# A hybrid GLA/Hyena layer with a mixture of experts: scale before shift, and the query between them

## The reference

```
mod = silu(cond) @ w_ada + b_ada            # w_ada: 2048 x 12288
sh1, sc1, gt1, sh2, sc2, gt2 = split(mod, 6)
h = rmsnorm(x, g_pre_mix) * (1 + sc1) + sh1
q, k, v, g, lr_f, lr_b, u_hy = split(h @ w_in)
la_f = log_sigmoid(lr_f @ w_dec_f + b) / 16      # likewise la_b
o = gla(q, k, v, la_f) + flip(gla(flip(...), la_b))   # chunks of 64, 4 heads
y_gla = rmsnorm(o) * silu(g);  y_hy = hyena(u_hy)     # long convolutions
x = x + gt1 * rmsnorm(concat(y_gla, y_hy) @ w_out, g_post_mix)
h = rmsnorm(x, g_pre_ffn) * (1 + sc2) + sh2
x = x + gt2 * rmsnorm(moe(h), g_post_ffn)        # 16 experts, top 2 of one group
```

## Time and profile before

| | |
|---|---|
| median of 3 runs | 1531.51 us (1527.08 to 1532.93) |
| profiled execution, its time | 1530.56 us |
| its span | 1528.7 us |
| PE busy | 1379.7 us (90%) |
| DVE busy | 748.8 us (49%) |
| ACT busy | 241.7 us (16%) |
| DMA traffic | 422.19 MB, mean 276 GB/s |
| mean granted PE clock | 0.965 |

### The profile page before, as it was taken

The page is one execution under the profiler, slowest core; times in us unless marked ns, Lnnn a source line. Parts: engine busy times, 40 slices in busy tenths (PEclk is TensorE's granted clock), DMA queues, the critical chain, the costliest instruction groups (busy, mean ns, idle before and its releaser), DMA issues.

```text
span 1528.7 us, 14045 instructions
## 1 busy us (share of the span) xinstructions
PE 1379.7 (90%) x5198; PEld 630.9 (41%) x5198; DVE 748.8 (49%) x1269; ACT 241.7 (16%) x401; POOL 75.1 (5%) x126
## 2 busy tenths in 40 slices
PE   2679999999999989999999999889989888798977
PEld 0135544444555545555544444543333333333322
DVE  0139889998677687978693752530000000000006
ACT  2110320100011111211121101521111101111104
POOL 3010000000001000000000001000000000000001
PEclk9689999999999999999999999989999999999999
DMA  9998458777549643322215844589999999999996
GB/s 345 424 359 254 170 173 276 249 259 254 165 144 339 222 146 109 117 69 90 83 55 213 289 157 170 235 351 427 427 426 394 430 427 428 426 386 427 427 424 279
DMA packets 134032, 422.19 MB, mean 276 GB/s; under 512 B 10253, under 2 KB 76024, under 8 KB 116852
## 3 DMA queue, kind: packets, MB, share of 16 engines
q1 hardware_dynamic: 120292, 375.79, 64.3%
q0 software_dynamic: 7584, 33.38, 6.0%
q10 hardware_dynamic: 6096, 12.20, 2.2%
HBM read 407.96 MB, written 22.58 MB: 282 GB/s over the span
## 4 chain that ended last, share of the span: by engine, by line
PE 74%; DMA 11%; DVE 8%; issue 3%; ACT 2%; ACTq 0%; POOL 0%; DVEq 0%; SPq 0%; POOLq 0%
PE ps L503 19%; PE ps L506 19%; PE ps L892 13%; PE ps L912 7%; DMA s_mem<-in_w_exp_gate 4%; PE ps L777 3%; DMA s_mem<-in_w_ada 3%; DMA s_mem<-in_w_exp_down 2%; DVE s_mem L1766 2%; PE ps L450 2%; PE ps L674 1%; DMA s_mem<-in_hy_freq 1%; PE ps L625 1%; PE ps L432 1%; DVE s_mem L1738 1%
## 5 line engine op out<-in xcount | busy, mean ns | idle before, releaser
L1592 DVE SCALAR_TENSOR_TENSOR s_mem<-s_mem,s_sT 128x512 f32<-128x512 f32 x480 | 339.4, 748 | 32.6 <-DMA s_mem<-in_w_ada 16.2
L503 PE MATMUL ps<-s_mem 128*128 128x384 f32 x1024 | 342.5, 492 | 1.1 <-DVE s_mem L1623 1.1
L506 PE MATMUL ps<-s_mem 128*128 128x512 f32 x672 | 292.8, 594 | 0.7 <-ACT s_mem L1366 0.7
L892 PE MATMUL ps<-s_mem 128*64 128x512 f32 x1152 | 256.4, 602 | 19.9 <-DMA s_mem<-in_w_exp_gate 18.7
L503 PEld LDWEIGHTS ps<-s_mem 128*128 128x128 f32 x1024 | 193.3, 191 | 142.5 <-issue 18.0
L506 PEld LDWEIGHTS ps<-s_mem 128*128 128x128 f32 x672 | 126.3, 190 | 158.5 <-issue 157.6
L892 PEld LDWEIGHTS ps<-s_mem 128*64 128x64 f32 x1152 | 87.4, 139 | 185.9 <-issue 185.9
L2059 DVE TENSOR_TENSOR s_mem<-s_mem,ps 64x512 f32<-64x512 f32 x18 | 12.2, 679 | 296.3 <-ACT s_mem L1461 296.3
L912 PE MATMUL ps<-s_mem 128*64 128x512 f32 x576 | 144.2, 659 | 9.3 <-DVE s_mem L2061 9.3
L1262 ACT ACTIVATE s_mem<-ps 128x512 f32<-128x512 f32 (+1 forms) x61 | 34.4, 581 | 316.3 <-PE ps L506 154.0
L912 PEld LDWEIGHTS ps<-s_mem 128*64 128x64 f32 x576 | 43.7, 150 | 96.4 <-issue 84.6
(11 more groups left out here) (287 smaller groups left out, 1025.0 us busy)
## 6 DMA issues: line engine op xcount, KB each, us to landing
s_mem<-in_w_ada SPq DMA_DIRECT2D x256, 256.0 KB, 3.2
s_mem<-in_w_exp_gate SPq DMA_DIRECT2D x32, 2048.0 KB, 21.1
s_mem<-in_w_exp_up SPq DMA_DIRECT2D x32, 2048.0 KB, 25.4
s_mem<-in_w_exp_down SPq DMA_DIRECT2D x32, 2048.0 KB, 24.4
s_mem<-in_w_in SPq DMA_DIRECT2D x24, 2048.0 KB, 8.8
s_mem<-in_w_ada SPq DMA_DIRECT2D x16, 2048.0 KB, 12.5
s_mem<-in_w_out SPq DMA_DIRECT2D x8, 2048.0 KB, 8.2
y_slots<-s_mem ACTq DMA_DIRECT2D x34, 256.0 KB, 11.1
```

The source lines that it names most:

```text
L503: m = mm(ps[:, banks[m_], 0:TOK], v[:, k, m_ * P:(m_ + 1) * P], hT[:, kk, :], start=(kk == 0), stop=(kk == KT - 1))
L506: m = mm(ps[:, banks[m_], :], hT[:, kk, m_ * P:(m_ + 1) * P], v[:, k, :], start=(kk == 0), stop=(kk == KT - 1))
L892: m = mm(ps[half, 0, :], hgT[:, kh * 8 + k, :], weights(e, 2 * kh + which)[:, k, :], start=(kh + k == 0), stop=(kh * 8 + k == KT - 1), ski ...
L1592: v.op(ve.scalar_tensor_tensor(out=o, in0=w, scalar=scale, in1=o, op0=ALU.mult, op1=ALU.add), S("piece_used") if last else None)
```

## The change

Scale and shift are separated. The scale comes first, in two halves of 1024 columns (four slots each, 4 k tiles by 1024 columns); then the shift in eight slots of 2 k tiles by 2048 columns. The query's two weight halves go to places of their own (`wq`) and no longer through the ring. PE multiplies the query weights with tokens that are scaled but not shifted, between the steps of the scale's second half and of the shift; the part of the query that comes from the shift is a separate product of the shift's columns with the query weights (`qshift`), turned to columns (`colQ`) and added by ACT as a bias when it copies the query out. The first half of the key now stands ahead of `lr`, and the decay products lie inside its second half. DVE scales tokens in two parts and adds the shift in a second pass. `run(26)` is gone; the pieces start after ring load 16 (the key's first half), and 13 more pieces stand among the loads of the output projection. The token loads come first on ACT's queue.

PE, new and changed:

```diff
-            pe.wait_ge(S("sT_ready"), 2)
-            for k in range(KT):
-                ada_step()
...
+            def scale_step(h, r):
+                cols = SCALE * D + 2 * h * NCOL
+                w = next_slot(pe, w_ada[4 * r * P:4 * (r + 1) * P, cols:cols + 2 * NCOL].rearrange("(k p) n -> p k n", p=P))
...
+            def shift_step(a):
+                w = next_slot(pe, w_ada[2 * a * P:2 * (a + 1) * P, SHIFT * D:(SHIFT + 1) * D].rearrange("(k p) n -> p k n", p=P))
...
+            def q_products(m_, kts):
+                for kt in kts:
+                    if m_ == 0:
+                        pe.wait_ge(S("h_scaled"), kt + 1)
+                    m = mm(ps[:, m_, 0:TOK], wq[kt // 8][:, kt % 8, m_ * P:(m_ + 1) * P], hT[:, kt, :],
+                           start=(kt == 0), stop=(kt == KT - 1))
+                return m
+
+            pe.wait_ge(S("sT_ready"), 2)
+            scale_step(0, 0)
+            scale_step(0, 1)
+            pe.wait_ge(S("x_scaled"), NT)
+            for kt in range(KT):
+                x_turn(kt)
+                if kt in (4, 9):
+                    scale_step(0, 2 + kt // 9)
+            scale_columns(0)
...
+            pe.wait_ge(S("in_q0"), 16)
+            for m_ in range(4):
+                take(pe, m_, f"q_{m_}", ("act",))
+                m = q_products(m_, range(8))
+                scale_step(1, m_)
+            m.then_inc(S("q_read"), 1)
+            shift_step(0)
+            scale_columns(1)
+            shift_step(1)
...
+            pe.wait_ge(S("in_q1"), 16)
+            for m_ in range(4):
+                m = q_products(m_, range(8, 12))
+                if m_ % 2 == 1:
+                    shift_step(2 + m_ // 2)
+            m.then_inc(S("q_read"), 1)
+            for m_ in range(2):
+                q_products(m_, range(12, KT)).then_inc(filled(f"q_{m_}"), 1)
+                shift_step(4 + m_)
+            shift_step(6)
+            shift_step(7)
+            q_products(2, range(12, KT)).then_inc(filled("q_2"), 1)
+            wait_read(pe, "dve", "shift")
+            mod_columns(SHIFT, 5)
+            q_products(3, range(12, KT)).then_inc(filled("q_3"), 1)
...
-            project("q", "fm", w_in, COL_Q)
-
+            where_k = ("k", "fm", w_in, COL_K)
+            project_half(*where_k, 0, between=q_shift_columns, banks=(4, 5, 7, 0))
+
+            pe.wait_ge(S("h_shifted"), KT)
             pe.wait_ge(S("in_lr"), 16)
-            take(pe, 4, "lr", ("act",))
+            take(pe, 3, "lr", ("act",))
...
+            def decay_products():
+                wait_read(pe, "act", "lr")
...
+                        if h % 2 == 1:
+                            yield
+
+            project_half(*where_k, 1, banks=(4, 5, 7, 0), turn=decay_products())
```

Where the sums stand, and SP:

```diff
-        ADA_SUMS = {("q", 1): 0, ("k", 1): 1, ("v0", 1): 2, ("v1", 0): 3, ("v1", 1): 4, ("g0", 0): 5, ("g0", 1): 6,
-                    ("g1", 0): 7, ("g1", 1): 8, ("hy00", 1): 9, ("hy01", 1): 10, ("hy10", 0): 12,
-                    ("wo1", 0): 13, ("wo2", 0): 14, ("wo2", 1): 15}
-        PIECES_AFTER = {1: 8, 2: 8, 3: 3, 4: 6, 5: 4, 6: 7, 7: 7, 8: 8, 9: 9, 10: 7, 11: 5, 12: 4, 13: 6, 14: 4,
-                        15: 6, 16: 4, 17: 8, 18: 2, 20: 2, 22: 2, 24: 2, 25: 4, 27: 4, 28: 6, 29: 2}
+        ADA_SUMS = {("v0", 0): 0, ("v0", 1): 1, ("v1", 0): 2, ("v1", 1): 3, ("g0", 0): 4, ("g0", 1): 5, ("g1", 1): 6,
+                    ("hy00", 1): 7, ("hy01", 1): 8, ("hy11", 0): 10, ("wo1", 0): 11, ("wo1", 1): 12, ("wo2", 0): 13,
+                    ("wo2", 1): 14}
+        PIECES_AFTER = {16: 4, 17: 1, 18: 3, 19: 5, 20: 7, 21: 8, 22: 9, 23: 9, 24: 8, 25: 5, 26: 4, 27: 6, 28: 4,
+                        29: 6, 30: 4, 31: 8, 32: 2, 34: 2, 36: 2, 38: 2, 39: 6, 40: 4, 41: 6, 42: 5, 43: 5, 44: 3}
...
+            def load_q(kh):
+
+                if kh == 1:
+                    sp.wait_ge(S("x_scaled"), NT)
+                sp.dma_start(wq[kh], w_block(w_in, kh * 8 * P, COL_Q)).then_inc(S(f"in_q{kh}"), 16)
...
-                if i == 0:
-                    small_loads()
-                for _ in range(PIECES_AFTER.get(i - KT, 0)):
+                if i in Q_LOAD_AFTER:
+                    load_q(Q_LOAD_AFTER[i])
+                for _ in range(PIECES_AFTER.get(i, 0)):
                     load_piece()
```

In the old table the keys count from the query's first half, in the new one from the list's start: new key n stands where old key n - 14 stood. `Q_LOAD_AFTER` is `{3: 0, 7: 1}`, and `small_loads` now comes before the list. DVE:

```diff
-            run(26)
...
-            mod_chunk(0)
             run(14)
...
-            mod_chunk(1)
             run(20)
+            mod_chunk(0)
+            mod_chunk(1)
+            run(16)
             mod_chunk(2)
             run(16)
             mod_chunk(3)
             mod_row(2)
+            run(20)
+            mod_chunk(4)
             run(16)
-            mod_chunk(4)
-            run(20)
             mod_chunk(5)
-            run(16)
-            mod_chunk(6)
             run(4)
...
-            mod_chunk(13)
+            run(10)
+            mod_chunk(11)
             mod_columns(3, 0)
...
                 if nb == 1:
-                    for _ in ada:
-                        pass
+                    run(16)
+                    mod_chunk(12)
+                if nb == 2:
+                    mod_chunk(13)
+                    run(6)
...
+                    if nb == 2 and t < 2:
+                        run(5)
```

More of the change, by code:

```diff
@@ L77, in shape_constants @@
     lower = (np.arange(P) >= BLK)[:, None]
-    base = np.concatenate([ident, tri, sel.reshape(P, 2 * P), total, np.tile(rows, (P, 1)), tokens, lower], 1).astype(np.float32)
+    shifts = np.zeros((P, 32), np.float32)
+    for j in range(4):
+        for c in range(2):
+            shifts[32 * j + 2 + c, c] = 1
+    base = np.concatenate([ident, tri, sel.reshape(P, 2 * P), total, np.tile(rows, (P, 1)), tokens, lower, shifts], 1).astype(np.float32)
     masks = np.zeros((P, 2, P), np.int32)
@@ new lines, in _ @@
+            for kt in range(KT):
[3 more added lines that the diff above has]
+            scale_columns(0)
+            pe.wait_ge(S("in_rowsB"), 32)
+            take(pe, 4, "colB")
+            tr(ps[:, 4, 0:96], rowsB, ident[0:96, 0:96]).then_inc(filled("colB"), 1)
+            pe.wait_ge(S("in_mlp"), 16 * 9)
+            take(pe, 3, "hid1")
+            mm(ps[0:HID, 3, 0:TOK], w1s, pe_sb, start=True, stop=True).then_inc(filled("hid1"), 1)
@@ new lines, in _ @@
+            wait_read(pe, "dve", "shift")
+            mod_columns(SHIFT, 5)
+            q_products(3, range(12, KT)).then_inc(filled("q_3"), 1)
+            wait_read(pe, "dve", "modT0")
+            take(pe, 6, "qshift", ("act",))
+            for k in range(KT):
+                j = k % 4
+                m = mm(ps[32 * j:32 * j + 32, 6, :], sT[:, k, :], wq[k // 8][:, k % 8, :], start=(k < 4),
+                       stop=(k >= KT - 4), skip_group_check=True)
+            m.then_inc(filled("qshift"), 1)
@@ L495, in project_half @@
                         take(pe, banks[m_], bk, readers)
-                    if m_ == 2 and between:
+                    if m_ == (1 if key == "k" else 2) and between:
                         between()
@@ L693, in _ @@
                 if ho == 0:
-                    project_half(*where, 0, both, turn=hy_turn(0, 1, (7, 7, 7), 11))
+                    project_half(*where, 0, both, turn=hy_turn(0, 1, (7, 7, 7), 9))
                 else:
@@ L785, in _ @@
             out_last(0, 1)
+            ada_sum(15)
             out_last(1, 0)
@@ L1212, in load @@
                 act.dma_start(dst, src).then_inc(S(sem), 16)
+            for t in range(NT):
+                load(x_sb[:, t, :], x_rows[t], f"in_x{t}")
             load(rowsB[0:72, :], T["hy_conv_w"][0].rearrange("j (m p) -> (j m) p", p=P), "in_rowsB")
@@ L1222, in _ @@
                 load(dst, src, "in_mlp")
-            for t in range(NT):
-                load(x_sb[:, t, :], x_rows[t], "in_x")
             wait_read(act, "dve", "colA")
@@ new lines, in _ @@
+            inverse_roots(0, NT)
+            for t in range(NT):
+                v.op(ve.tensor_scalar(h_tm[:, t, :], x_sb[:, t, :], stat[:, t:t + 1], None, ALU.mult), S("x_scaled"))
+            dve.wait_ge(S("in_rows"), 16 * 10)
+            scale_tokens(0)
+            b = read(dve, "colB")
+            v.op(ve.tensor_copy(colB[:, :], ps[:, b, 0:96]), freed("dve", "colB"))
+            dve.wait_ge(S("in_mlp"), 16 * 9)
+            sine_argument("hid1", 0, HID)
+            scale_tokens(1)
@@ L1628, in _ @@
+                for c, toks in both:
+                    v.op(ve.tensor_scalar(hT[:, kt, toks], hT[:, kt, toks], sT[:, kt, 2 + c:3 + c], None, ALU.add),
+                         S("h_shifted") if c == 1 else None)
             for d in range(2):
@@ L1839, in _ @@
             gla_head(2)
-            mod_chunk(9)
+            mod_chunk(7)
             gla_head(3)
```

215 lines of the change are left out of this document (116 added, 99 removed).

## The result

The changed kernel takes 1561.2 us (median of 4 runs, 1558.9 to 1563.0); the kernel before took 1529.95 beside it. The ratio is 1.0203, 95% interval 1.0186 to 1.0221: 31 us slower, where 1530 and a range of 1516 to 1543 had been predicted. The direction and the range were both wrong.

The account below looks back on a forecast made before the run. Transfers were taken to bound the prologue, then DVE's chain from the last decay product to the first head. Terms: -0.1 us at the head, -1.2 in the output projection, -1.3 in all; forecast 1530 us, range 1516 to 1543.

Parts of the forecast that it names:

- E: Moment when the last decay product ends on PE; predicted at 164.8 us, against 161.9 in the kernel before.
- the head: Start of `g1`'s second half, beside which the first linear-attention head runs; predicted at 359.8 us, against 359.9 before.
- The 35 us of my last section: Expected trace sign: PE idle at L432, released by L1592, some 35 us between E and the head.
- The 4.9 us wait: DVE's one long idle, for an exponential queued behind the last key copy; predicted to go.
- the slower rival: In the prologue, PE waits for scaled tokens and the query starts at 54.5; 1539 to 1540 us, chance 0.22.
- an ada step is 1.92 us at the higher clock, 3.6 at the lower: Price per ada step on PE in the prologue, set by PE's clock.
- the prologue is a transfer: Claim that loads of 33.5 MB bound the prologue; last shift load taken at 107.3 us.
- the tail to the key: PE's work from the last shift load to the key's start; predicted 9.7 us, key at 117.
- PE waits at `ada_sum`, blocked until its chunk is ready: Between E and the head, PE's own work is 157 us and it waits for DVE's chunks.
- DVE is idle during the key instead, some 40 us: DVE idles some 40 us beside the key, since pieces begin only after the last decay product.
- The first rival: DVE's chain does not set the head, PE does: head at 334.8, 25 us earlier, 1504 us; chance 0.10.
- my own last paragraph: Expected trace signs, among them the key's first matmul at 117 us (109 to 126).

Follow-up runs that it names:

- e4_low_rank_in_key: Changed kernel with the low-rank product after the key's first block and decay products after its next blocks; 1546.8 us.
- e1_four_groups: Changed kernel with the scale step alternating over all four 32-column groups, DVE adding the second partial sum; 1551.4 us.
- e2_bank_freed_early: Changed kernel with `mod_chunk(0)`, which frees the PSUM bank, ahead of `run(20)` instead of behind it; 1555.7 us.
- e5: As e3, with the first value third `v0` accumulating in banks 3, 1 and 2 instead of 0, 1 and 2; 1515.4 us.
- e7_queries_ahead_of_last_loads: As e5 plus the four-group scale step of e1_four_groups, and the last two query pieces ahead of the last two shift steps; 1503.1 us.
- e3: Changed kernel with 26 `w_ada` steps and their loads moved ahead of and between the decay additions, and `mod_chunk(0)` early; 1528.9 us.

## Why the prediction was wrong, step by step

**Right.** DVE's chain from E sets the head in the main (e4_low_rank_in_key moved E by 14.9 and the head by 15.6). DVE idles beside the key: it waited 45.2 us at L1742, 29.6 of them at once. PE waits at the ada sums in its place: 24.8 us in three waits before the head. (The 35 us of my last section don't fit my own sum: 195.0 less PE's own 157 leaves 38, of which 13 were the `v0` load's.) The `v0` load comes at E + 14.8 (13 predicted). Chunk 0 is complete at E + 39.9 (39.6 predicted). The 4.9 us wait ahead of the key preparation is gone. The tokens did not gate the query, so the slower rival named the wrong mechanism: all tokens were scaled at 24.8 us (23 to 25 predicted). The query began at 47.0, the edge of what I had allowed, because PE was busy with slow steps until then. The output projection hid its 26 additional steps; this is DVE ahead of its last block, where 10 us of slack had been predicted:

```profile
973.17 0.69 DVE L2001 TENSOR_TENSOR s_mem<-s_mem,ps 128x512 f32<-128x512 f32 x1 [9.95 <-PE ps L852]
```

**The failed step: "an ada step is 1.92 us at the higher clock, 3.6 at the lower".** I read the 3.59 us of the earlier trace rows as the clock's (granted 0.52 in 98.9 to 102.4 us, 1.00 in 62.7 to 64.6) and gave the scale's new step 1.92, without looking on which partitions it writes. Both prices are right for that layout, but the new step takes 3.63 us at a granted clock of 1.00, by its own layout on two column groups. 8 steps x 1.7 us made PE later than the loads, against my "the prologue is a transfer". That moved the key, and with it E, the head and the end. e1_four_groups gives 10 us for this term alone. It is the largest single term and not the whole: so repaired, the kernel takes 1551.4 us, still above the range. Its span is 21.4 us above the forecast: the last load is used 5.9 us late, the tail to the key is 2.9 longer, key to E 2.7, E to head 4.7, head to end 5.3.

**Sizes of the same kind.** The query-shift product was put at 1.9 us as if it had 16 instructions; it has 32 (16 k tiles, one matmul each, two instructions a matmul): 3.64. The rest of the tail is the low clock behind the waits for loads (step 3.64, third block's quarter 3.96, which is 2.85 in e1_four_groups). The decay products come in four pairs of 1.3 us, 5.2 us, not 3.1: 2.1 of the 2.7 us between key and E. After the repair of the step, the last load is still used at 113.2 and not at 107.3. The queues ran at 410 GB/s in 40 to 80 us where I had counted 432 for the ring's slots; over 18 loads of 2.1 MB that is 37.7/0.410 - 37.7/0.432 = 4.6 us of the 5.9. That this is the shorter rows' doing was argued and not tested.

**The missed wait.** "PE waits at `ada_sum`, blocked until its chunk is ready" has two conditions, and I followed one. The sum also needs its bank, and DVE frees that in `mod_chunk(0)`, now behind 20 more steps. 8.5 us of PE at this point, 4.6 at the head (e2_bank_freed_early). With it, DVE waited 4.6 us for a piece at 303.3 and 3.9 us for PE at the head, neither of which stood in my list.

**The sum without these.** Even with key and chain as predicted, the change would have been no gain. Of the 28.4 us by which the span grew over the kernel before, 24.1 are E's (186.0 against 161.9), 2.4 are the stretch from E to the head, and 1.9 come behind it. Both kernels do 110 steps between E and the head. The 26 steps of `run(26)` did find a place, in the output projection, where they cost nothing. What stayed unused is in my own text: "DVE is idle during the key instead, some 40 us". I took this as a fact of the change, and did not ask which of the 110 steps could stand there. 26 of them are 38.4 us of DVE's chain; put beside the key, with the bank freed early, they brought 32.3 us. The first rival ("the query is really hidden", 25 us earlier) had chance 0.10; what it gives was reached here once the steps stood in that gap and the bank was swapped (e5). e5_value_off_bank_0 goes 14.9 us below the kernel before, and e7_queries_ahead_of_last_loads 27 us (ratio 0.9826).

**Chances.** Slower had 0.22, all of it for one mishap with the tokens. The range ended at 1543, since I let each term of the prologue vary alone; key start could have been 126 by my own last paragraph, which alone gives 1539, and the step's length had no bound from above, although no row showed a step on two groups.

## What to carry to other kernels

When the order of the projections changes, ask for each engine where it now stands idle ahead of its own chain, and which steps of that chain could be done there: 26 steps beside the key were worth more here than the whole change. When a step is cut into another shape, price it by its layout on the array (which 32-column groups in turn, how many instructions), not by the old row with the same shape. For a wait on a filled buffer, look up both conditions, data ready and bank free, and follow who frees the bank.

## What the runs showed of the hardware

- Sixteen matmul instructions of 128x32 by 512 columns take 3.63 us when they go in turn to two of the four 32-column groups and 1.92 us when they go to four, at the same granted clock of 1.00. Thirty-two on four groups take 3.64.
- Between key and head the same work took PE some 5 us more busy time at a mean granted clock of 0.92 than at 1.00 (210.05 against 204.72 us). A half of 48 matmul instructions took 23.31 us behind a wait of 14.8 us (granted clock 0.89), and 20.8 at 1.00.
- The last shift step took 3.25 to 3.64 us behind waits of 1.9 to 3.1 us, in the changed kernel and six experiments; in e7_queries_ahead_of_last_loads, where query products filled the wait to 0.3 us, it took 1.92.
- The same wait does not always have this price. The step ahead of it stood behind a wait of 3.04 or 3.05 us in five kernels whose prologue is the same, and took 1.92 (e2, e4, e5), 2.64 (e3) and 3.12 us (the changed kernel). Its row in e5_value_off_bank_0:

```profile
117.17 1.92 PE L459 MATMUL ps<-s_mem,s_sT 128*32 128x512 f32 x16 [3.05 <-DMA s_mem<-in_w_ada]
```
